# A hybrid attention and mLSTM layer on eight cores: finished mLSTM rows transposed by DMA, from four row buffers

## The chip, the cores and the metric

The kernel runs on the 8 cores of one Trainium2 chip. Each core works through 3 of the 24 sequences alone; the cores share nothing but the memory outside. The metric is the device time in microseconds of the slowest core. A core has TensorE (PE; its weight loads are PEld), VectorE (DVE), ScalarE (ACT), GpSimd (POOL) and SyncE (SP), which here issues nearly all DMAs. Each engine runs its own instructions in order and waits on semaphores for the others.

## The reference

One layer over x of 2048 tokens by 2048 columns per sequence. Cut to what matters:

```python
h = rmsnorm(x, norm_g); proj = h @ w_in            # 6672 columns
# group A: 8 query heads, 2 kv heads, QK norm, rotary positions, softmax attention, times silu(az)
# group B: 4 mLSTM heads, q/k 128 wide, v 256 wide, chunks of 128 tokens, one scan per direction
h_fwd = mlstm_chunkwise(mq, mk, mv, i_f, log_sigmoid(f_f))
h_bwd = flip(mlstm_chunkwise(flip(mq), flip(mk), flip(mv), flip(i_b), flip(log_sigmoid(f_b))))
hm = sigmoid(mo) * (h_fwd + h_bwd)                 # (B, S, 4 heads, 256)
hm = rmsnorm(hm, mlstm_norm_g)                     # per head, weights of 256 columns per head
mlstm_out = hm * silu(mz)
y = concatenate([attn_out, mlstm_out]) @ w_out     # 2048 x 2048
return x + y
```

## The kernel before

A sequence passes through `first_pass` and `attention` (group A), then for each of the 4 mLSTM heads a state stage (`mlstm_states`) and an output stage (`mlstm_out`), then `out_proj`. The normed input stands transposed in `hT`. `mixT` is [128, 16, 2048]: rows 0 to 7 receive the attention output and rows 8 to 15 the mLSTM output, both transposed (column of the mixer on the partition, token along the row), since `out_proj` uses them as stationary operands. The rest of the work uses `arena`, from which tiles are carved by byte offset, and the rows of `mixT` not yet written.

An output stage (L1018 on) runs over 16 chunks c of 128 tokens. Per chunk TensorE computes `front(c+1)` (the scores, L1024, and the forward state update, L1027), `numer(c)` (four matmuls into two banks, L1058 and L1061) and `fin(c)` (the projection to the output gate and the z gate, 16 matmuls of 512 columns, L1094, into bank 6 or 7 by c % 2). Around them:

- VectorE masks the scores (L1032, twice), updates the state (L1043), takes the denominators (L1072 to L1074) and adds the two directions (L1080), all for the numerator; then for the gates L1110 and L1111 (step f1; L1111 is the last reader of the projection's bank), the norm's mean (L1118) and the product of row, norm factor and gate (L1124, step f4) into the row buffer `ob`.
- ScalarE scales the first numerator (L1077, which waits for L1074 and for which L1080 waits), takes the tanh of the projection (L1107, f0), the sum of squares of the gated row into `ob` (L1114, f2, after L1110) and, after the transpose, copies the two halves to `mixT` with the norm's weights `gmcol` as per-partition scale (L1133, f5).
- GpSimd converts the state (L1045) and takes the root (L1120).

What sets the order: the kernel is written out by a planner, the class `Flow`. It holds a clock, `F.now`, which advances by fixed costs when TensorE's work is written (T512 = 217, T256 = 111, T128 = 64 ns), and a list of steps with due times. `F.chain` puts the steps of `fin` at sums of the given distances from the end of its projection; `F.due()`, called ahead of each group of TensorE's work, writes the steps that are due. The order in which instructions are written is the order on each engine, DMAs on SP included. `Sched` (`S`) derives the waits from the tiles read and written; two readers of one PSUM bank count as dependent.

State stages (L932 on) project q, k, v and build the backward states. In the first two sequences those of heads 0 to 2 also carry the prenorm of the next sequence (`prenorm`): SP loads a block of 128 rows of x to one of two buffers `xf` in rows 12 to 15 of `mixT`, nine us later by the planner L450 on ScalarE squares it, and the normed block is stored to `xnd`. Behind L450 on ScalarE stand L954 and L994, which empty the projections' banks. In the first sequence each weight tile is also saved as bf16 (`w_get`, 4 us after its first use) and the next is loaded 1.5 us after the old one is released (`w_rel`).

`out_proj` loads the rows of x to be added into four tiles `xres`, the first four at its start, and writes y through four tiles `ysb`.

Of the kernel before, what the change touches and what calls it, by code (L numbers as in the profile page):

```python
# [7 lines left out]
F32 = mybir.dt.float32  # L8
BF16 = mybir.dt.bfloat16
ALU = mybir.AluOpType  # L10
AF = mybir.ActivationFunctionType
# [202 lines left out]
NT = SEQ // 128  # L214
# [30 lines left out]
T512, T256, T128 = 217.0, 111.0, 64.0  # L245
# [41 lines left out]
def build_program(nseq=SEQ_PER_CORE):  # L287
# [21 lines left out]
    with ExitStack() as es:  # L309
        S = Sched(nc, es)  # L310
        F = Flow()
# [3 lines left out]
        mixT = S.sb("mixT", [128, KC, SEQ], BF16)  # L315
# [27 lines left out]
        def bankb(i):  # L343
            return PP[i // 2].bitcast(BF16)[:, 1024 * (i % 2):1024 * (i % 2) + 1024]
# [4 lines left out]
        def carve(region, off, shape, dt):  # L349
            n = int(np.prod(shape[1:]))  # L350
            nb = n * (4 if dt == F32 else 2)
            base, size = (arflat, ARENA) if region == 'ar' else (mixflat, 65536)
            assert off % 4 == 0 and off + nb <= size, (region, off, nb)
            v = base[:, off // 2:(off + nb) // 2]
            if dt == F32:
                v = v.bitcast(F32)
            if len(shape) == 3:
                v = v.rearrange("p (a b) -> p a b", a=shape[1])
            elif len(shape) == 4:
                v = v.rearrange("p (a b c) -> p a b c", a=shape[1], b=shape[2])  # L360
            return Tile(v, region, off, nb)
# [4 lines left out]
        def mk(r, t0, t1):  # L366
            return ['mx.%d' % (16 * r + t) for t in range(t0, t1)]
# [549 lines left out]
        kxb = [carve('ar', 19968 + 256 * i, [128, 128], BF16) for i in range(4)]  # L917
        Pm = [[carve('ar', 20992 + 512 * i + 256 * d, [128, 128], BF16) for d in range(2)] for i in range(2)]
        Csf = [carve('ar', 22016 + 768 * i, [128, 257], BF16) for i in range(2)]
        ob = [carve('ar', 23552 + 512 * i, [128, 256], BF16) for i in range(2)]  # L920
        soz = [carve('ar', 24576 + 2048 * i, [128, 512], F32) for i in range(2)]
        hA = [carve('ar', 28672 + 1024 * i, [128, 256], F32) for i in range(2)]
        Uf = carve('ar', 39936, [128, 257], F32)
# [2 lines left out]
        def csl(c):  # L926
            return slice(c * 128, (c + 1) * 128)
# [90 lines left out]
        def mlstm_out(s_, h):  # L1018
# [65 lines left out]
            def fin(c):  # L1084
# [26 lines left out]
                    S.op('dve', lambda: V.scalar_tensor_tensor(zo, zo, 1.0, bank(b)[:, 256:512], ALU.add, ALU.mult), reads=[kz, bn], writes=[kz])  # L1111

                def f2():
                    S.op('act', lambda: A.activation(ob[i].ap, oo, AF.Square, accum_out=st[:, 64 + i:65 + i]), reads=[ko],  # L1114
                         writes=[ob[i], 'ssm%d' % i])

                def f3():
                    S.op('dve', lambda: V.tensor_scalar(st[:, 66 + i:67 + i], st[:, 64 + i:65 + i], 1.0 / 64, 16.0 * EPS, ALU.mult, ALU.add),  # L1118
# [2 lines left out]
                         reads=['rlm%d' % i, 'const'], writes=['rsm%d' % i])  # L1121

                def f4():
                    S.op('dve', lambda: V.scalar_tensor_tensor(ob[i].ap, oo, st[:, 68 + i:69 + i], zo, ALU.mult, ALU.mult),  # L1124
                         reads=[ko, kz, 'rsm%d' % i], writes=[ob[i]])

                def f5():
                    tp = bankb(5)
                    S.group('pe', [(lambda k=k: P.transpose(tp[:, 128 * k:128 * k + 128], ob[i].ap[:, 128 * k:128 * k + 128], identb))
                                   for k in range(2)], reads=[ob[i], 'const'], writes=['B5'])  # L1130
                    F.now += 2 * T128
                    for k in range(2):
                        S.op('act', lambda k=k: A.activation(mixT[:, 8 + 2 * h + k, csl(c)], tp[:, 128 * k:128 * k + 128], AF.Copy,  # L1133
                                                             scale=gmcol[:, 2 * h + k:2 * h + k + 1]),
                             reads=['B5', 'constg'], writes=mk(8 + 2 * h + k, c, c + 1))
                F.chain((100, f0), (700 if c > 0 else 1700, f1), (600, f2), (800, f3), (2000, f4), (3600, f5))

            for c in range(NT):
                F.due()
# [5 lines left out]
            w_rel(('OZ%d' % h, s_))  # L1145


        xres = [carve('ar', 30720 + 2048 * i, [128, 512], F32) for i in range(4)]
        ysb = [carve('ar', 2048 * i, [128, 512], F32) for i in range(4)]

        def out_proj(s_):
# [148 lines left out]
```

How the kernel before makes its waits and increments, by code:

```python
    def _wait(self, eng, need):  # L93
        kn = self.known[eng]
        changed = False
        for s, v in need.items():
            if kn.get(s, 0) >= v:
                continue
            if eng == 'pe' and s.startswith('pe_e'):
                continue
            self.E[eng].wait_ge(self.sems[s], v)
            if not changed:
                kn = dict(kn)
                changed = True
            kn[s] = v
            sn = self.snap.get((s, v))
            if sn is not None:
                for s2, v2 in sn.items():
                    if kn.get(s2, 0) < v2:
                        kn[s2] = v2
        if changed:
            self.known[eng] = kn
# [16 lines left out]
    def group(self, eng, fns, reads=(), writes=()):  # L129
        reads, writes = self._bankify(reads, writes)
        self._wait(eng, self._deps(reads, writes))
        sname = "%s_e%d" % (eng, self.epoch[eng])
        sem = self.sem(sname)
        ins = None
        for fn in fns:
            ins = fn()
        ins.then_inc(sem, 1)
        self.cnt[sname] += 1
        ticket = (sname, self.cnt[sname])
        self.snap[ticket] = self.known[eng]
        if self.cnt[sname] >= self.EPOCH:
            self.epoch[eng] += 1
        self._commit(ticket, reads, writes)
        return ticket
# [4 lines left out]
    def dmas(self, eng, pairs, reads=(), writes=(), sem='dma', **kw):  # L149
# [2 lines left out]
        s = self.sem(sem)  # L152
        for (o, i) in pairs:
            self.E[eng].dma_start(out=o, in_=i, **kw).then_inc(s, 16)
            self.cnt[sem] += 16
```

## Time and profile before

| | before |
|---|---|
| median of 3 runs | 4069.55 us (4062.42 to 4496.65) |
| the profiled execution, its own time | 4081.78 us |
| its span on the slowest core (6) | 4080.4 us |
| spans of the 8 cores | 4044.2 to 4080.4 us |
| mean granted TensorE clock of the cores | 0.991 to 0.995 |
| busy: TensorE, VectorE, ScalarE, GpSimd | 96%, 47%, 40%, 23% |
| DMA queue of SP, share of 16 engines | 26.9% |
| L1129, transposes on TensorE | 384, 52.8 us busy |
| L1133, scaled copies on ScalarE | 384, 140.1 us busy |

The profile is of one execution on the slowest core. A line number such as L1094 is the line of the kernel before. Busy time of an engine is the union of its recorded intervals; consecutive instructions overlap, so the distance of two starts says what one costs its engine, and the recorded duration how long it lasts by itself. A wait behind an instruction names who ended the idle time ahead of it.

### The profile page before, as it was taken

Reading aid. Unit: us, or ns where it says so; the run is one execution under the profiler, and the core shown is the slowest. Engines: PE = TensorE matmul, PEld = TensorE weight load, DVE = VectorE, ACT = ScalarE, POOL = GpSimd, SP = SyncE. Lnnn points to the kernel's source line nnn. Section 1 sums busy time; section 2 is a strip of 40 time slices with the busy share of each in tenths; the row PEclk is TensorE's granted clock in tenths of the full one; section 3 lists DMA queues with packets and bytes.
Section 4 is the critical chain, followed back from the end, with each engine's and each line's share of the span. In section 5 each row is a group of like instructions: output and inputs, shape, how many; then the busy total and the mean of one; then the engine's idle time right before and its main releaser. Section 6 shows DMA issues by size and latency. Waiting matters only on the chain.

```text
span 4080.4 us, 72076 instructions; the slowest of 8 cores (4044.2 to 4080.4 us)
## 1 busy us (share of the span) xinstructions
PE 3915.4 (96%) x23590; PEld 2045.7 (50%) x23590; DVE 1928.4 (47%) x4961; ACT 1630.0 (40%) x3479; POOL 947.1 (23%) x1301
## 2 busy tenths in 40 slices
PE   4799899999999999999999999999999999999999
PEld 2444454565554445445456655444544446665544
DVE  3654454455552245445455555224545445555521
ACT  3464456344330026555644433003655563233300
POOL 2443330122210053333021211005333311111100
PEclk8999999999999999999999999999999999999999
DMA  8344410643319931011023211993101100110264
GB/s 220 81 80 67 76 46 20 198 124 110 89 50 219 228 109 30 23 36 36 38 98 120 99 42 47 213 234 92 38 15 35 36 22 22 42 42 22 76 190 149
DMA packets 199342, 358.34 MB, mean 88 GB/s; under 512 B 81088, under 2 KB 130624, under 8 KB 184384
## 3 DMA queue, kind: packets, MB, share of 16 engines
q1 hardware_dynamic: 182768, 318.01, 26.9%
q0 software_dynamic: 16208, 35.72, 6.0%
q8 instruction: 197, 3.23, 0.3%
q14 instruction: 169, 1.38, 0.1%
HBM read 278.25 MB, written 102.76 MB: 93 GB/s over the span
## 4 chain that ended last, share of the span: by engine, by line
PE 83%; DMA 5%; SPq 4%; DVE 3%; issue 3%; ACT 2%; POOL 1%; DVEq 0%; ACTq 0%; POOLq 0%
PE PP L1094 16%; PE PP L1190 12%; PE PP L680 10%; PE PP L762 8%; PE PP L724 8%; PE PP L775 7%; PE PP L947 7%; PE PP L988 6%; SPq L154 4%; PE PP L800 2%; DMA xnd<-arena 1%; DMA arena<-c_rope 1%; PE PP L1058 1%; PE PP L1061 1%; DMA y<-arena 1%
## 5 line engine op out<-in xcount | busy, mean ns | idle before, releaser
L769 ACT ACTIVATE arena<-PP 128x1024 bf16<-128x1024 f32 x768 | 770.4, 1025 | 154.5 <-PE PP L762 153.1
L1094 PE MATMUL PP<-WR,hT 128*128 128x512 bf16 x3072 | 696.2, 379 | 0.2
L1190 PE MATMUL PP<-WR,mixT 128*128 128x512 bf16 x3072 | 669.5, 381 | 9.7 <-DVE arena L1163 9.6
L680 PE MATMUL PP<-WR,hT 128*128 128x512 bf16 (+1 forms) x3072 | 571.5, 328 | 11.1 <-DMA WR<-w_A 9.9
L1190 PEld LDWEIGHTS PP<-WR,mixT 128*128 128x128 bf16 x3072 | 300.8, 98 | 374.8 <-issue 18.7
L762 PE MATMUL PP<-mixT 128*128 128x512 bf16 x1536 | 458.9, 381 | 7.6 <-ACT arena L769 6.4
L775 PE MATMUL PP<-arena,mixT 128*128 128x512 bf16 x1536 | 458.4, 380 | 2.3 <-ACT arena L769 2.3
L1094 PEld LDWEIGHTS PP<-WR,hT 128*128 128x128 bf16 x3072 | 298.7, 98 | 320.5 <-issue 1.0
L724 PE MATMUL PP<-hT,WR 128*128 128x512 bf16 x1536 | 409.8, 382 | 34.7 <-DMA WR<-w_Z 21.9
L680 PEld LDWEIGHTS PP<-WR,hT 128*128 128x128 bf16 x3072 | 298.3, 98 | 244.6 <-issue 15.8
L658 POOL TENSOR_TENSOR mixT<-arena 128x384 f32<-128x384 f32 (+1 forms) x192 | 196.3, 1023 | 907.8 <-DVE arena L639 869.2
L1163 DVE TENSOR_TENSOR arena<-PP,arena 128x512 f32<-128x512 f32 x192 | 132.6, 691 | 517.7 <-PE PP L1190 375.2
L988 PE MATMUL PP<-WR,hT 128*128 128x256 bf16 x3072 | 362.8, 274 | 0.0
L947 PE MATMUL PP<-hT,WR 128*128 128x512 bf16 x1536 | 353.7, 379 | 0.0
L988 PEld LDWEIGHTS PP<-WR,hT 128*128 128x128 bf16 x3072 | 295.4, 98 | 44.2
L649 ACT CAST mixT<-PP 128x128 bf16<-128x128 f32 x96 | 25.6, 266 | 704.5 <-DVE arena L639 677.9
L724 PEld LDWEIGHTS PP<-hT,WR 128*128 128x128 bf16 x1536 | 146.2, 98 | 206.2 <-issue 47.3
L762 PEld LDWEIGHTS PP<-mixT 128*128 128x128 bf16 x1536 | 132.9, 98 | 208.6 <-issue 85.3
L669 POOL TENSOR_TENSOR stats<-stats,ccol 128x3 f32<-128x3 f32 (+1 forms) x192 | 174.4, 909 | 241.8 <-DVE stats L667 239.4
L947 PEld LDWEIGHTS PP<-hT,WR 128*128 128x128 bf16 x1536 | 147.3, 98 | 155.6 <-issue 1.3
L642 ACT ACTIVATE mixT<-PP 128x128 bf16<-128x128 f32 x480 | 134.3, 280 | 203.2 <-DVE arena L639 177.6
L843 POOL TENSOR_TENSOR mixT<-arena 128x512 bf16<-128x512 f32 x90 | 116.8, 1297 | 409.4 <-DVE arena L839 392.4
(156 smaller groups left out, 4438.0 us busy)
## 6 DMA issues: line engine op xcount, KB each, us to landing
arena<-x SPq DMA_DIRECT2D x192, 256.0 KB, 5.0
y<-arena SPq DMA_DIRECT2D x192, 256.0 KB, 5.2
mixT<-x SPq DMA_DIRECT2D x38, 1024.0 KB, 7.0
arena<-c_rope SPq DMA_DIRECT2D x192, 128.0 KB, 2.0
WR<-wd_OUT SPq DMA_DIRECT2D x12, 2048.0 KB, 9.7
xnd<-arena SPq DMA_DIRECT2D x32, 512.0 KB, 2.9
WR<-wd_QKV SPq DMA_DIRECT2D x8, 2048.0 KB, 8.2
WR<-wd_OZ SPq DMA_DIRECT2D x8, 2048.0 KB, 8.1
```

Source lines behind the costliest of these rows:

```text
L154: self.E[eng].dma_start(out=o, in_=i, **kw).then_inc(s, 16)
L658: S.op('pool', lambda: G.tensor_tensor(t23.rearrange("p h (r f e) -> p (h r) f e", r=2, f=2), xrot, tab[r].ap[:, 1:2, :].to_broadcast([128 ...
L669: S.op('pool', lambda: G.tensor_tensor(st[:, c_rs:c_rs + nh], st[:, c_rl:c_rl + nh], nhalf.to_broadcast([128, nh]), ALU.pow), reads=['rlq% ...
L680: S.group('pe', [(lambda kc=kc: P.matmul(pv[:, 0:ncol], hT[:, kc, T * 128:(T + 1) * 128], W[:, kc, c0:c0 + ncol], start=(kc == 0), stop=(k ...
L724: S.group('pe', [(lambda kc=kc: P.matmul(bank(b), W[:, kc, c0:c0 + 128], hT[:, kc, qb * 512:(qb + 1) * 512], start=(kc == 0), stop=(kc == ...
L762: S.group('pe', [(lambda u=u: P.matmul(pr_[:, 512 * u:512 * (u + 1)], kt.ap[:, (2 * j + u) * 128:(2 * j + u + 1) * 128], qt.ap[:, hh, qb * ...
L769: S.op('act', lambda: A.activation(PT[t % NPT].ap, spair[t % 2][:, 0:1024], AF.Exp, scale=128.0 ** -0.5), reads=spn[t % 2], writes=[PT[t % ...
L775: S.group('pe', [(lambda u=u: P.matmul(bank(4), vs.ap[:, 2 * j + u, :], pt.ap[:, 512 * u:512 * (u + 1)], start=(j == 0 and u == 0), stop=( ...
L947: S.group('pe', [(lambda kc=kc: P.matmul(bank(b), W[:, kc, 128 * which:128 * which + 128], hT[:, kc, ts], start=(kc == 0), stop=(kc == KC ...
L988: S.group('pe', [(lambda kc=kc: P.matmul(bank(b)[:, 0:256], hT[:, kc, csl(c)], W[:, kc, 256:512], start=(kc == 0), stop=(kc == KC - 1))) f ...
L1094: S.group('pe', [(lambda kc=kc: P.matmul(bank(b), hT[:, kc, csl(c)], W[:, kc, 0:512], start=(kc == 0), stop=(kc == KC - 1))) for kc in ran ...
L1190: S.group('pe', [(lambda kc=kc: P.matmul(bank(b), mixT[:, kc, csl(T)], W[:, kc, 0:512], start=(kc == 0), stop=(kc == KC - 1))) for kc in r ...
```

## The change

Step f5 no longer transposes on TensorE. It issues two DMA transposes from SP (128x128 each, from the row buffer to the two rows of `mixT`), and no longer multiplies by the norm's weights. A new step f6, once every four chunks, multiplies four chunks of each of the two rows (128x512) in place on ScalarE, 12 us by the planner after the DMAs of the fourth (22 us after those of the last chunk). So that a row can wait for its DMA, the row buffer `ob` has four copies in place of two; the two new ones take bytes 30720 to 31743 of `arena`, and the `xres` tiles of `out_proj` move from 30720 to 8192. f5 is due 0.7 us after f4 (3.6 us before), and the planner's clock no longer advances by 2 x T128 for the transposes.

```diff
-        ob = [carve('ar', 23552 + 512 * i, [128, 256], BF16) for i in range(2)]
+        ob = [carve('ar', o, [128, 256], BF16) for o in (23552, 24064, 30720, 31232)]
...
                 def f2():
-                    S.op('act', lambda: A.activation(ob[i].ap, oo, AF.Square, accum_out=st[:, 64 + i:65 + i]), reads=[ko],
-                         writes=[ob[i], 'ssm%d' % i])
+                    S.op('act', lambda: A.activation(ob[c % 4].ap, oo, AF.Square, accum_out=st[:, 64 + i:65 + i]), reads=[ko],
+                         writes=[ob[c % 4], 'ssm%d' % i])
...
                 def f4():
-                    S.op('dve', lambda: V.scalar_tensor_tensor(ob[i].ap, oo, st[:, 68 + i:69 + i], zo, ALU.mult, ALU.mult),
-                         reads=[ko, kz, 'rsm%d' % i], writes=[ob[i]])
+                    S.op('dve', lambda: V.scalar_tensor_tensor(ob[c % 4].ap, oo, st[:, 68 + i:69 + i], zo, ALU.mult, ALU.mult),
+                         reads=[ko, kz, 'rsm%d' % i], writes=[ob[c % 4]])
 
                 def f5():
-                    tp = bankb(5)
-                    S.group('pe', [(lambda k=k: P.transpose(tp[:, 128 * k:128 * k + 128], ob[i].ap[:, 128 * k:128 * k + 128], identb))
-                                   for k in range(2)], reads=[ob[i], 'const'], writes=['B5'])
-                    F.now += 2 * T128
+                    S.dmas('sp', [(mixT[:, 8 + 2 * h + k, csl(c)], ob[c % 4].ap[:, 128 * k:128 * k + 128]) for k in range(2)],
+                           reads=[ob[c % 4]], writes=mk(8 + 2 * h, c, c + 1) + mk(9 + 2 * h, c, c + 1), sem='ox%d' % (c % 4),
+                           transpose=True)
+
+                def f6():
                     for k in range(2):
-                        S.op('act', lambda k=k: A.activation(mixT[:, 8 + 2 * h + k, csl(c)], tp[:, 128 * k:128 * k + 128], AF.Copy,
-                                                             scale=gmcol[:, 2 * h + k:2 * h + k + 1]),
-                             reads=['B5', 'constg'], writes=mk(8 + 2 * h + k, c, c + 1))
-                F.chain((100, f0), (700 if c > 0 else 1700, f1), (600, f2), (800, f3), (2000, f4), (3600, f5))
+                        row = 8 + 2 * h + k
+                        S.op('act', lambda row=row: A.activation(mixT[:, row, 128 * c - 384:128 * c + 128], mixT[:, row, 128 * c - 384:128 * c + 128],
+                                                                 AF.Copy, scale=gmcol[:, row - 8:row - 7]),
+                             reads=['constg'], writes=mk(row, c - 3, c + 1))
+                F.chain((100, f0), (700 if c > 0 else 1700, f1), (600, f2), (800, f3), (2000, f4), (700, f5), *([(12000 if c < NT - 1 else 22000, f6)] if c % 4 == 3 else []))
...
-        xres = [carve('ar', 30720 + 2048 * i, [128, 512], F32) for i in range(4)]
+        xres = [carve('ar', 8192 + 2048 * i, [128, 512], F32) for i in range(4)]
```

The order on VectorE in the middle of an output stage, before, one chunk (a line number, the operation, output<-input):

```order
L1080 SCALAR_TENSOR_TENSOR arena<-PP,stats,arena 128x256
L1124 SCALAR_TENSOR_TENSOR arena<-arena,stats 128x256
L1032 SCALAR_TENSOR_TENSOR arena<-PP,g_eX,cb 128x128 x2
L1043 SCALAR_TENSOR_TENSOR arena<-arena,g_lam,PP 128x257
L1110 SCALAR_TENSOR_TENSOR arena<-arena 128x256
L1111 SCALAR_TENSOR_TENSOR arena<-arena,PP 128x256
L1072 TENSOR_TENSOR stats<-PP,g_thr 128x2
L1073 SCALAR_TENSOR_TENSOR stats<-PP,stats 128x2
L1074 RECIPROCAL stats<-stats 128x2
L1118 TENSOR_SCALAR stats<-stats 128x1
```

And of the change, at the same place (the lines up to L1129 have the same numbers in both):

```order
L1080 SCALAR_TENSOR_TENSOR arena<-PP,stats,arena 128x256
L1118 TENSOR_SCALAR stats<-stats 128x1
L1032 SCALAR_TENSOR_TENSOR arena<-PP,g_eX,cb 128x128 x2
L1043 SCALAR_TENSOR_TENSOR arena<-arena,g_lam,PP 128x257
L1124 SCALAR_TENSOR_TENSOR arena<-arena,stats 128x256
L1072 TENSOR_TENSOR stats<-PP,g_thr 128x2
L1073 SCALAR_TENSOR_TENSOR stats<-PP,stats 128x2
L1074 RECIPROCAL stats<-stats 128x2
L1110 SCALAR_TENSOR_TENSOR arena<-arena 128x256
L1111 SCALAR_TENSOR_TENSOR arena<-arena,PP 128x256
```

L1124 moved behind the front's three instructions, L1110 and L1111 behind L1072 to L1074, and L1118 behind L1080. The first chunks of a stage have this order in both kernels.

On SP, from the end of head 0's state stage to the first blocks of head 1's in sequence 0, the difference of the two orders (`mixT<-x` is a load of the prenorm, `wd_OZ` and `wd_QKV` are saves of weights):

```order
 L154 DMA xnd<-arena 128x2048 x2
 L154 DMA wd_OZ<-WR 128x8192
+L154 DMA_TRANSPOSE mixT<-arena 128x128 x30
 L154 DMA mixT<-x 128x2048
 L154 DMA wd_QKV<-WR 128x8192
+L154 DMA_TRANSPOSE mixT<-arena 128x128 x2
 L154 DMA mixT<-x 128x2048
 L154 DMA xnd<-arena 128x2048
```

Nothing stood between the save and the two loads of the prenorm before; now the transposes of fifteen chunks stand ahead of the first load and those of the sixteenth ahead of the second.

## Rows read from the trace of the kernel before

**Rows 1.** The page: busy time, share of the span, instructions
```profile
PE 3915.4 (96%) x23590; PEld 2045.7 (50%) x23590; DVE 1928.4 (47%) x4961; ACT 1630.0 (40%) x3479; POOL 947.1 (23%) x1301
```

**Rows 2.** Lines by form: xcount, busy us, mean ns, idle before and releaser
```profile
L1133 ACT ACTIVATE mixT<-PP,gmcol 128x128 bf16<-128x128 bf16 x384 | 140.1, 365 | 65.0 <-PE PP L1129 45.2 <-ACT mixT L1133 0.4
...
L1107 ACT ACTIVATE arena<-PP 128x512 f32<-128x512 f32 x192 | 113.2, 590 | 39.8 <-PE PP L1094 39.7
...
L1114 ACT ACTIVATE arena<-arena 128x256 bf16<-128x256 f32 x192 | 79.9, 416 | 291.2 <-DVE arena L1110 289.4 <-DVE arena L1111 1.8
...
L1129 PE MATMUL PP<-cb,arena 128*128 128x128 bf16 x384 | 52.8, 219 | 0.0
```

**Rows 3.** TensorE in order of time, middle chunk: start, us, instruction
```profile
943.20 0.28 PE L1129 MATMUL PP<-cb,arena 128*128 128x128 bf16 x2
943.31 0.22 PE L1024 MATMUL PP<-arena 128*128 128x128 bf16 x1
...
943.92 3.62 PE L1094 MATMUL PP<-WR,hT 128*128 128x512 bf16 x16
...
948.09 3.62 PE L1094 MATMUL PP<-WR,hT 128*128 128x512 bf16 x16
```

**Rows 4.** VectorE in order of time, middle stretch [idle before <-releaser]
```profile
944.50 0.48 DVE L1080 SCALAR_TENSOR_TENSOR arena<-PP,stats,arena 128x256 f32<-128x256 f32 x1 [0.59 <-ACT arena L1077]
...
948.63 0.49 DVE L1080 SCALAR_TENSOR_TENSOR arena<-PP,stats,arena 128x256 f32<-128x256 f32 x1 [0.59 <-ACT arena L1077]
```

**Rows 5.** VectorE in order of time, early in the same stage
```profile
918.55 0.48 DVE L1080 SCALAR_TENSOR_TENSOR arena<-PP,stats,arena 128x256 f32<-128x256 f32 x1 [0.35 <-ACT arena L1077]
...
920.38 0.48 DVE L1124 SCALAR_TENSOR_TENSOR arena<-arena,stats 128x256 bf16<-128x256 f32 x1
...
921.40 0.42 DVE L1110 SCALAR_TENSOR_TENSOR arena<-arena 128x256 f32<-128x256 f32 x1
921.75 0.41 DVE L1111 SCALAR_TENSOR_TENSOR arena<-arena,PP 128x256 f32<-128x256 f32 x1
922.91 0.48 DVE L1080 SCALAR_TENSOR_TENSOR arena<-PP,stats,arena 128x256 f32<-128x256 f32 x1 [0.74 <-ACT arena L1077]
```

**Rows 6.** ScalarE in order of time, the same early stretch
```profile
921.92 0.42 ACT L1114 ACTIVATE arena<-arena 128x256 bf16<-128x256 f32 x1 [1.98 <-DVE arena L1110]
...
922.34 0.46 ACT L1077 ACTIVATE arena<-PP,stats 128x256 f32<-128x256 f32 x1
```

**Rows 7.** TensorE in order of time, third projection of that stage
```profile
914.69 3.61 PE L1094 MATMUL PP<-WR,hT 128*128 128x512 bf16 x16
```

**Rows 8.** The tensor xnd: ns on SP, min/median/max, and time to landing
```profile
L154 SPq DMA_TRANSPOSE hT<-xnd x32: 2279/5948/12349, 1225.2 to 2713.6; - x32
...
DMA to landing us min/median/max: 2.7/5.4/16.1
```

**Rows 9.** SP in order of time, from 700 us: loads of x rows
```profile
708.72 0.33 SPq L154 DMA_DIRECT2D mixT<-x  x1
...
777.12 0.79 SPq L154 DMA_DIRECT2D mixT<-x  x1
...
801.34 0.43 SPq L154 DMA_DIRECT2D mixT<-x  x1
```

**Rows 10.** DMA issues, 708.7 to 709: KB, us to landing
```profile
mixT<-x SPq DMA_DIRECT2D x1, 1024.0 KB, 26.3
```

**Rows 11.** TensorE in order of time, in head 0's state stage
```profile
741.13 0.26 PE L961 MATMUL PP<-cb,arena 128*128 128x128 bf16 x1 [5.91 <-DVE arena L968]
```

**Rows 12.** State stages: window, length, busy by engine, PEclk, DMA share, GB/s
```profile
709.50:779.20 69.70, 62.25 (x429) 41.30 (x426) 26.65 (x67) 25.79 (x37) 11.53 (x23) 0.95 0.67 199
845.50:906.00 60.50, 59.19 (x423) 39.79 (x421) 24.40 (x66) 26.12 (x44) 10.95 (x22) 1.00 0.59 183
...
2033.60:2098.10 64.50, 59.67 (x429) 39.73 (x426) 26.75 (x68) 25.79 (x37) 11.30 (x22) 1.00 0.43 164
2164.60:2224.60 60.00, 58.98 (x424) 39.98 (x422) 24.19 (x66) 26.13 (x44) 10.44 (x21) 1.00 0.45 167
```

## The prediction

> **What bounds the kernel now.** I read the page first. The reader is to see that TensorE is busy 96% of the span [rows 1]: time goes if TensorE gets less to do, and comes if it is made to wait. Then the grouped lines [rows 2] for the sizes of what is removed, and the engines in order of time in one middle stretch of `mlstm_out`. There TensorE goes from one output projection to the next in 948.09 - 943.92 = 4.17 us without a gap [rows 3]. That is a chunk; there are 16 in a stage, 12 stages (4 heads, 3 sequences), 192 in all. Then VectorE in the same stretch: from one L1080 to the next it takes 948.63 - 944.50 = 4.13 us, and its only idle time is 0.59 us, for ScalarE's L1077 [rows 4]. So VectorE is busy or waiting on a chain of its own all the time, only 0.04 us per chunk ahead of TensorE. That second fact decides the forecast.
>
> **Part 1, the transposes on TensorE go.** Two L1129 start at 943.20 and the next matmul at 943.31 [rows 3]: 0.11 us per chunk, 0.055 each. 384 of them: 384 x 0.055 = 21.1 us of TensorE's time, all on the path. A chunk then needs 4.17 - 0.11 = 4.06 us of TensorE.
>
> The Trainium skill ("TensorE: Matmul & The Clock Gate", Part 4) gives about 275 ns for such a transpose within a kernel, with access latency as most of it; by that the part would be worth 106 us. The trace does not agree: it records 219 ns for one as a duration [rows 2], but the next matmul starts 55 ns later.
>
> **Part 2, ScalarE.** Out go 384 L1133 of 365 ns (140.1 us, [rows 2]); in come 96 scalings of 128x512 from SBUF. Their size isn't in the trace: between 416 ns (L1114, half the elements) and 590 ns (L1107, as many, from PSUM) [rows 2]. I take 590, the nearest in size: 57 us. ScalarE isn't the bound. The two scalings stand behind a tanh (L1107) and ahead of a square (L1114) that waits for VectorE anyway (the 192 L1114 wait 289.4 us for L1110, [rows 2]), so 1.2 us every fourth chunk costs nothing. Without that cover it would be 48 x 1.2 = 57 us of ScalarE, which TensorE sees only past a chunk of lag.
>
> **Part 3, the order on VectorE turns.** The order is made by the planner's clock. With 128 ns less per chunk its chunk is shorter than the 4200 ns to step f4, so L1124 and L1110/L1111 fall behind the next chunk's front (L1032, L1043) and its L1072 to L1074, in every middle chunk. The order rows show it. This order can be priced, because the kernel before runs it once in the first chunks of a stage [rows 5]: L1080, L1118, L1032 twice, L1043, L1124, L1072 to L1074, L1110 (921.40), L1111 (921.75), L1080 (922.91). From L1080 at 918.55 to the next at 922.91 are 4.36 us. Why longer with the same instructions: L1080 waits for ScalarE's L1077, which now stands behind the square L1114, which waits for L1110; so VectorE finishes L1111 and idles 0.74 us where it idled 0.59, and L1118, which used to fill part of the wait before it, comes behind [rows 5, 6]. Nothing in that loop waits for TensorE. So the chain needs 4.36 us per chunk and TensorE 4.06: VectorE falls back 0.30 us per chunk.
>
> What is late next: L1111 frees the PSUM bank that the projection two chunks on writes. In the early stretch it is done at 921.75 + 0.41 = 922.16; without the transposes that projection would start at 914.69 + 2 x 4.06 = 922.81, against 923.03 now [rows 5, 7]. The lead is 0.65 us at the fifth projection, and goes at 0.30 per chunk: it is used up by the seventh. Nine more chunks then run at 4.36: 9 x 0.30 = 2.7 us per stage, 12 x 2.7 = 32 us given back, more than part 1 brought. Bounds: 0, if the records hide slack that I don't see, and 0.30 x 13 = 3.9 per stage (47 us), if no lead is left at chunk 3.
>
> **Part 4, the transposes on the DMA queue.** A DMA transpose from SBUF isn't in the trace; the nearest is `hT<-xnd`, 16 times as large, which holds SP at least 2.28 us [rows 8]. Lower bound for SP: 0.33 us, a plain DMA's issue [rows 9]. If the part above 0.33 goes with size it is 0.33 + 1.95 / 16 = 0.45 us; I take 0.5, so 1 us of SP per chunk of 4.06 to 4.36. For landing I take 3 us, between the bounds 2.7 and 16.1 of `xnd`'s transfers [rows 8] and near the lower, since the queue is nearly empty in an output stage. The row buffer is needed again by L1114 four chunks later. L1114 runs at 921.92 and its L1124 one turn after 920.38, at 924.74 [rows 5, 6], so 4 x 4.36 - 2.8 = 14.6 us remain; the scaling waits for a landing at least 12 us old by the planner. Both are hidden except behind a burst of weights.
>
> The Trainium skill ("VectorE: DVE Perf Modes", The three transpose paths) has 1309 ns for the DMA transpose of 128x128 against 390 ns on TensorE, and its rules say to use TensorE where PSUM will do. By its figure two take 2.6 us of each chunk's 4.06 and the sum stays as it is; no run here shows it yet.
>
> **Part 5, SP is in order.** Before, SP ran ahead: the first two loads of x rows for the next state stage went out at 777.12 and 801.34, tens of us before the stage began at 845.5 [rows 9, 12]. Now each stands behind the transposes of a whole output stage, which wait for L1124; the first goes out just after the state stage begins, the second behind the last chunk's pair, some 5 us in, with the stage's weights (and in sequence 0 the save of weights) ahead of it. The prenorm's L450 on ScalarE waits for them, and behind L450 stand the evictions that TensorE needs. The stage of head 0 shows the price, since there the loads go out that late already: one issued at 708.72 took 26.3 us to land [rows 9, 10], TensorE stood 5.9 us behind it, and the granted clock of the stage was 0.95 in the mean; it took 69.7 us against 60.5 for head 1's [rows 11, 12]. In sequence 1: 64.5 against 60.0 [rows 12]. The change can bring heads 1 and 2 of sequences 0 and 1 to this level: at most 2 x 9.2 + 2 x 4.5 = 27 us, at least 0. I take two thirds of the first and half of the second, because the first load still lands in time: 12 + 4.5 = 16 us. Head 3 and sequence 2 have no such loads.
>
> The move of `xres` makes all four first loads wait for the last numerator matmul; two did so before. They land before the fourth step needs its bank: 0.
>
> **The sum.** -21 + 32 + 16 = +27 us. The profiled execution's own time is 4081.8 (span 4080.4): it would be 4109. The median of the runs shown is 4069.55, 12 us less: forecast 4096 us, 0.6% slower. (2% is 81 us, about what a measurement of this kernel can tell from no change: under 3988 is faster, over 4151 slower.)
>
> **The rivals.**
> - *Only part 3, the x loads stay hidden* (4096 - 16 = 4080). For: the first load has 9 us by the plan. Against: head 0. Chance 0.20.
> - *Neither*: the gain stays, 4069.6 - 21 = 4048. Needs a loop that doesn't reach TensorE; against it is the 4.36 in the trace. Chance 0.14. *Only part 5*: 4064, chance 0.08.
> - *SP becomes the bound*: if a small transpose holds SP as long as the large one's minimum, a chunk needs 2 x 2.28 = 4.56 us of SP; against 4.17 now that is 0.39 x 192 = 75 us, and with part 5 4069.6 + 75 + 16 = 4160, slower by over 2%. It decides from 2.03 us per transpose on (4.06 / 2). Landings over 14.6 us would do the same through L1114. For: each row is a short packet. Against: the large one has 16 times the rows. Chance 0.07.
> - *A transpose is worth its recorded duration*: 384 x 0.219 [rows 2] = 84 us, 3985 us. Against: the 55 ns step. Chance 0.01. The page "TensorE: Matmul & The Clock Gate" of the Trainium skill goes this way, with its 275 ns.
> - The forecast: 0.50, its own range 4072 to 4125.
>
> **How the numbers follow.** Everything but the last two rivals lies within 2%: faster 0.01, same 0.92, slower 0.07. The range goes from the gain kept (4048, and 2 us of scatter) to the forecast with both bounds high (-21 + 47 + 27 = 53: 4123, and 5 us for landings behind the weights): 4046 to 4128. It leaves out the last two rivals, a tail of the forecast and half of *neither*: about 0.17.
>
> **What would show it.** In the profile after: TensorE's chunk 4.06 us at the start of an output stage and about 4.36 at its end, with waits of L1094 or L1058 for L1111 or L1080 of about 0.3 us; VectorE's step from L1080 to L1080 4.36 us with an idle time of 0.74; no wait of L1114 for a DMA in most chunks; SP under 1 us per pair; `mixT<-x` for heads 1 and 2 issued after the stage's start, those stages 63 to 70 us. Wrong would be: chunks of 4.06 us to the end of the stage (part 3 falls), state stages of 60.5 (part 5 falls), or transposes of over 2 us on SP.

## The result, and the profile after

| | before | after |
|---|---|---|
| median of the runs | 4069.55 us | 4144.36 us |
| ratio of the comparable runs, 95% interval | | 1.0162 [1.0129, 1.0194] |
| the profiled execution: span of core 6 | 4080.4 us | 4143.2 us |
| its output stages, 12 together | 796.9 us | 819.9 us |
| its state stages, 12 together | 729.7 us | 768.0 us |
| its attention group, 3 together | 1837.1 us | 1832.0 us |
| its `out_proj`, 3 together | 679.0 us | 685.8 us |

The change made the kernel 1.6% slower, where 0.6% was forecast, and 4144 us lies above the range. Of the three runs after, one (4312.6 us) had a die at a lower clock and is left out of the ratio. A stage is counted from TensorE's first matmul in it to its first in the next, the first attention group from its first projection, the last `out_proj` to TensorE's last matmul.

The table is of the slowest core. From the kernel before to the change, each of the eight cores takes 22.5 to 28.0 us more in its output stages and 25.5 to 38.3 us more in its state stages. In `out_proj` seven cores had 663.9 us before; after, the eight have 663.2 to 694.8.

The page after, busy time of the engines and the chain that ended last, answers [rows 1]:

```profile
PE 3890.5 (94%) x22807; PEld 2018.0 (49%) x23206; DVE 1930.1 (47%) x4961; ACT 1549.4 (37%) x3191; POOL 954.9 (23%) x1301
...
PE 68%; DVE 8%; SPq 7%; issue 7%; DMA 6%; ACT 3%; POOL 1%; DVEq 0%; ACTq 0%; POOLq 0%
```

TensorE has 25 us less to do and stands idle 88 us longer. Three groups of instructions of after, by form (xcount | busy, mean ns | idle before, releaser), answer [rows 2]; the last line is from the same view:

```profile
L1094 PE MATMUL PP<-WR,hT 128*128 128x512 bf16 x2988 | 687.6, 379 | 33.3 <-DVE arena L1111 26.3
...
L1114 ACT ACTIVATE arena<-arena 128x256 bf16<-128x256 f32 x192 | 80.0, 417 | 450.6 <-DVE arena L1110 437.0
...
L1135 ACT ACTIVATE mixT<-mixT,gmcol 128x512 bf16<-128x512 bf16 x96 | 63.7, 714 | 54.5 <-DMA mixT<-arena 54.5
```

The wait of L1094 for L1111 is the forecast one; before, L1094 had 0.2 us of idle time ahead of it in all. TensorE's waits of after (releaser: us, times, longest us) name the second place:

```profile
PE PP L973 <- ACT arena L994: 36.5, 10, 10.3
...
PE PP L1094 <- DVE arena L1111: 26.3, 87, 0.7
```

**Output stage.** TensorE in order of time, head 1 of sequence 0 (start, us; answers [rows 3, 7]):

```profile
933.61 3.62 PE L1094 MATMUL PP<-WR,hT 128*128 128x512 bf16 x15
...
937.67 3.62 PE L1094 MATMUL PP<-WR,hT 128*128 128x512 bf16 x16
...
946.27 3.61 PE L1094 MATMUL PP<-WR,hT 128*128 128x512 bf16 x16 [0.20 <-DVE arena L1111]
...
950.68 3.61 PE L1094 MATMUL PP<-WR,hT 128*128 128x512 bf16 x16 [0.20 <-DVE arena L1111]
```

A chunk takes 937.67 - 933.61 = 4.06 us while TensorE has its lead, and 4.41 once it waits. VectorE over one such chunk (answers [rows 4, 5]) has the forecast order and a slightly larger idle time:

```profile
946.92 0.48 DVE L1080 SCALAR_TENSOR_TENSOR arena<-PP,stats,arena 128x256 f32<-128x256 f32 x1 [0.80 <-ACT arena L1077]
...
949.78 0.42 DVE L1110 SCALAR_TENSOR_TENSOR arena<-arena 128x256 f32<-128x256 f32 x1
950.12 0.41 DVE L1111 SCALAR_TENSOR_TENSOR arena<-arena,PP 128x256 f32<-128x256 f32 x1
951.34 0.48 DVE L1080 SCALAR_TENSOR_TENSOR arena<-PP,stats,arena 128x256 f32<-128x256 f32 x1 [0.80 <-ACT arena L1077]
```

**State stage.** Windows of after: head 1's state stage and output stage in sequence 0, head 1's state stage in sequence 1 (columns as in [rows 12]):

```profile
842.42:917.02 74.60, 60.76 (x414) 40.30 (x417) 24.90 (x68) 27.11 (x45) 11.22 (x22) 0.93 0.67 193
917.02:985.30 68.28, 65.61 (x341) 32.45 (x347) 47.49 (x168) 23.30 (x64) 16.19 (x32) 1.00 0.22 45
2191.68:2260.05 68.37, 61.27 (x414) 40.25 (x418) 24.86 (x68) 27.00 (x45) 10.64 (x21) 0.95 0.44 151
```

They were 60.5, 66.3 and 60.0 us. SP, ScalarE and TensorE around the start of the first of them, in order of time (three answers; SP's rows answer [rows 9]):

```profile
785.83 62.30 SPq L154 DMA_TRANSPOSE mixT<-arena  x30
848.18 0.59 SPq L154 DMA_DIRECT2D mixT<-x  x1
848.88 0.60 SPq L154 DMA_DIRECT2D wd_QKV<-WR  x1
849.57 2.49 SPq L154 DMA_TRANSPOSE mixT<-arena  x2
852.11 1.36 SPq L154 DMA_DIRECT2D mixT<-x  x1
...
865.60 1.91 ACT L450 ACTIVATE arena<-mixT 128x2048 bf16<-128x2048 f32 x1 [12.10 <-DMA mixT<-x]
...
868.00 0.37 PE L973 MATMUL PP<-arena 128*128 128x257 bf16 x1 [10.33 <-ACT arena L994]
```

The first load leaves 5.8 us into the stage and lands some 17 us later; L450 waits for it, L994 stands behind L450, and TensorE behind L994. The save of the QKV weights, at 801 us before, leaves right behind that load.

### The profile page after: what moved, and what is told of

Same layout as the page of the kernel before. It is cut to its first block, busy times and chain, and to the rows that moved or that the text cites. A ratio compares the mean times of both kernels' runs of the same rounds, so it can differ in the third digit from the quotient of the medians.

```text
span 4143.2 us, 70724 instructions; the slowest of 8 cores (4099.1 to 4143.2 us)
## 1 busy us (share of the span) xinstructions
PE 3890.5 (94%) x22807; PEld 2018.0 (49%) x23206; DVE 1930.1 (47%) x4961; ACT 1549.4 (37%) x3191; POOL 954.9 (23%) x1301
## 2 busy tenths in 40 slices
DMA packets 260778, 370.90 MB, mean 90 GB/s; under 512 B 142528, under 2 KB 192064, under 8 KB 245824
## 4 chain that ended last, share of the span: by engine, by line
PE 68%; DVE 8%; SPq 7%; issue 7%; DMA 6%; ACT 3%; POOL 1%; DVEq 0%; ACTq 0%; POOLq 0%
PE PP L680 10%; PE PP L1192 9%; PE PP L1094 9%; PE PP L762 8%; PE PP L724 7%; PE PP L775 7%; SPq L154 7%; PE PP L947 6%; PE PP L988 6%; PE PP L800 2%; DMA mixT<-x 2%; DVE arena L1032 2%; DVE arena L1124 1%; DMA xnd<-arena 1%; DMA arena<-c_rope 1%
## 5 line engine op out<-in xcount | busy, mean ns | idle before, releaser
L1094 PE MATMUL PP<-WR,hT 128*128 128x512 bf16 x2988 | 687.6, 379 | 33.3 <-DVE arena L1111 26.3
L1094 PEld LDWEIGHTS PP<-WR,hT 128*128 128x128 bf16 x3072 | 290.8, 97 | 374.1 <-issue 56.5
L762 PE MATMUL PP<-mixT 128*128 128x512 bf16 x1463 | 441.9, 380 | 15.7 <-ACT arena L769 6.3
L775 PE MATMUL PP<-arena,mixT 128*128 128x512 bf16 x1473 | 444.1, 380 | 5.9 <-ACT arena L769 2.3
L1165 DVE TENSOR_TENSOR arena<-PP,arena 128x512 f32<-128x512 f32 x192 | 132.8, 692 | 523.2 <-DMA y<-arena 262.4
L947 PE MATMUL PP<-hT,WR 128*128 128x512 bf16 x1488 | 353.8, 386 | 2.5
L1114 ACT ACTIVATE arena<-arena 128x256 bf16<-128x256 f32 x192 | 80.0, 417 | 450.6 <-DVE arena L1110 437.0
L947 PEld LDWEIGHTS PP<-hT,WR 128*128 128x128 bf16 x1536 | 150.5, 99 | 166.0 <-issue 11.9
L1120 POOL TENSOR_TENSOR stats<-stats,ccol 128x1 f32<-128x1 f32 x192 | 105.7, 551 | 479.2 <-DVE stats L1118 462.9
```

Of the source, the lines that this page charges most:

```text
L762: S.group('pe', [(lambda u=u: P.matmul(pr_[:, 512 * u:512 * (u + 1)], kt.ap[:, (2 * j + u) * 128:(2 * j + u + 1) * 128], qt.ap[:, hh, qb * ...
L775: S.group('pe', [(lambda u=u: P.matmul(bank(4), vs.ap[:, 2 * j + u, :], pt.ap[:, 512 * u:512 * (u + 1)], start=(j == 0 and u == 0), stop=( ...
L947: S.group('pe', [(lambda kc=kc: P.matmul(bank(b), W[:, kc, 128 * which:128 * which + 128], hT[:, kc, ts], start=(kc == 0), stop=(kc == KC ...
L1094: S.group('pe', [(lambda kc=kc: P.matmul(bank(b), hT[:, kc, csl(c)], W[:, kc, 0:512], start=(kc == 0), stop=(kc == KC - 1))) for kc in ran ...
```

## Experiments

Stage sums below are of core 6 of each profiled execution. The kernel before has 796.9 us in output stages and 729.7 in state stages, of which heads 1 and 2 have 60.5 and 61.1 in sequence 0, 59.9 and 59.7 in sequence 1.

**VectorE's order of before, on the changed kernel.**

```diff
                     transpose=True)
+                    F.now += 2 * T128
...
-                F.chain(... (2000, f4), (700, f5), ... 12000 if c < NT - 1 else 22000, f6
+                F.chain(... (2000, f4), (3600, f5), ... 9100 if c < NT - 1 else 19100, f6
```

> The change with the planner's clock of the kernel before: f5 due 3.6 us after f4 and the clock advanced by 128 ns in f5, f6 2.9 us earlier after f5. VectorE and ScalarE then have exactly the order of before, without L1133. Theory (VectorE's order costs the output stages): each output stage falls from 68.3 us to between 65.5 and 66.2, the 12 together 25 to 33 us, so a ratio to before of about 1.008 in place of 1.016; the state stages of heads 1 and 2 stay long (the loads of x stand behind the transposes still), perhaps a few us better. Rival (the transposes on SP or their transfers cost the output stages by themselves): output stages stay at 68, ratio 1.016.

Ratio 1.0074 [1.0050, 1.0099]. The output stages are 794.3 us together: the whole +23 us of them is gone. The state stages take 747.0, so 17 us of their +38 stay. In sequence 1 they are 61.6 and 59.9, in sequence 0 72.2 and 72.5.

**The order alone, on the kernel before.**

```diff
-                    F.now += 2 * T128
```

> The kernel before, transposes on TensorE, with only the planner's clock not advanced for them: the order on VectorE turns as in the change, SP as before. Theory: VectorE's loop of 4.36 us paces the chunks above TensorE's 4.17, so output stages of 66.3 us grow to 67.5 to 68.8, 12 of them 15 to 30 us, ratio 1.004 to 1.007; state stages unchanged. Rival (the order doesn't matter): ratio 1.000.

Ratio 1.0109 [1.0074, 1.0144]; output stages 818.8 us, 68.2 each, state stages 731.9. The stages are as expected. The ratio is above the expected 1.004 to 1.007: the stages of core 6 add up to 24 us, 0.6%, and the rest lies in the slowest cores of the two longer of its four executions (4116.3 and 4120.0 us; the profiled one took 4091.4). It isn't explained. This kernel issues no DMA transpose in them and its TensorE still does the work of before. VectorE's loop ends as in the change (start, us, idle before):

```profile
949.37 0.48 DVE L1080 SCALAR_TENSOR_TENSOR arena<-PP,stats,arena 128x256 f32<-128x256 f32 x1 [0.75 <-ACT arena L1077]
...
953.74 0.48 DVE L1080 SCALAR_TENSOR_TENSOR arena<-PP,stats,arena 128x256 f32<-128x256 f32 x1 [0.75 <-ACT arena L1077]
```

With the transposes on TensorE and without them the stage takes 68.2 to 68.3 us: once the loop over VectorE and ScalarE sets the chunk, at 4.36 to 4.37 us here, what TensorE is spared doesn't count.

**The planner's clock restored and nothing else.**

```diff
                     transpose=True)
+                    F.now += 2 * T128
```

> The change with one line added: the planner's clock advances by 2 x T128 behind the DMA transposes, as it did behind TensorE's. Nothing else of the work differs. Theory (order on VectorE): the steps fall to other places again, L1124 now directly behind L1118, of which it needs GpSimd's root; each chunk then waits 0.8 us more and takes about 5.2 us, output stages 75 to 79 us, ratio 1.03 to 1.04 above the change, 1.04 to 1.05 above the kernel before. Rival (the DMA transposes or the copies make the output stages long, whatever the order): output stages 68 us as in the change.

The profiled execution took 4253.7 us, 109 more than the change; output stages 78.0 to 78.8 us, 940.2 together. VectorE in order of time there:

```profile
931.45 0.48 DVE L1080 SCALAR_TENSOR_TENSOR arena<-PP,stats,arena 128x256 f32<-128x256 f32 x1 [0.35 <-ACT arena L1077]
931.85 0.14 DVE L1118 TENSOR_SCALAR stats<-stats 128x1 f32<-128x1 f32 x1
932.80 0.48 DVE L1124 SCALAR_TENSOR_TENSOR arena<-arena,stats 128x256 bf16<-128x256 f32 x1 [0.80 <-POOL stats L1120]
...
936.63 0.48 DVE L1080 SCALAR_TENSOR_TENSOR arena<-PP,stats,arena 128x256 f32<-128x256 f32 x1 [0.74 <-ACT arena L1077]
```

L1124 stands behind L1118 and waits 0.80 us for GpSimd's root; the chunk takes 5.18 us. The same instructions in three orders gave output stages of 66, 68 and 78 us. So the order is what sets them.

**The first two loads early**, written 30 us into the output stage ahead (heads 1 and 2, first two sequences).

```diff
...
             W, wk, _ = w_get(('OZ%d' % h, s_))
+            if s_ + 1 < nseq and h < 2:
+                for n in range(2):
+                    F.after(30000 + 100 * n, lambda n=n: xf_load(s_ + 1, n + (6, 11)[h]))
```

> The change, with the first two loads of x for heads 1 and 2 written 30 us into the output stage before (in sequences 0 and 1), so ahead of that stage's last transposes on SP. Theory (late loads cost the state stages): those four state stages fall from 74.6, 73.6, 68.4 and 68.3 us to 60 to 61, together about 43 us, output stages unchanged at 68.3; ratio about 1.006. Rival (the transfers of the transposes slow those stages): they stay at 68 to 75, ratio 1.016.

Ratio 1.0102 [1.0081, 1.0124]; state stages 733.2 us. Sequence 1 is back at 59.9 and 59.5; sequence 0 has 65.9 and 65.2, still 4 to 5 over. So the theory holds in sequence 1 and falls short in sequence 0, and the ratio is above the expected 1.006. Part of that lies in `out_proj`, where the three slowest cores of this run took 669.3 to 674.4 us.

**Both: order of before and early loads.** The two edits above together.

> Both undone: the clock of before and the early loads, transposes still by DMA. Theory: the two repairs add up, -30 and -43 us from the change's +66: ratio 0.997 to 0.999, output stages 65.5 to 66.2, state stages 59 to 61. Rival (something else in the DMA transposes costs 30 us or more): ratio 1.005 or more.

Ratio 1.0070 [1.0048, 1.0092]: not as expected. Output stages 794.2 as they should be, state stages 736.7, since sequence 0 still has 68.3 and 65.3. ScalarE shows a wait there that I had not priced (in this kernel L450 has its old number):

```profile
868.01 1.91 ACT L450 ACTIVATE arena<-mixT 128x2048 bf16<-128x2048 f32 x1 [6.83 <-DMA xnd<-arena]
```

It is the second block's L450, which waits until the first block is stored. That store took 8.8 us to land, 3.9 before. Beside it ran the save of 2 MB, issued 5 us into the stage. The rest of the distance to the kernel before lies in the slowest cores of this run (core 0 has a mean granted clock of 0.984) and isn't explained.

**Loads and save early.** The two edits together, and the save moved as well:

```diff
...
+            if s_ == 0 and nseq > 1 and h < 2:
+                F.after(40000, lambda: w_save(('QKV%d' % (h + 1), 0)))
```

> The change with VectorE's order of before, the first two x loads of heads 1 and 2 written 30 us into the output stage ahead of them, and the save of the QKV weights of heads 1 and 2 written 40 us into it. The run with the loads alone moved kept state stages of 64 to 71 us for heads 1 and 2 of the first sequence, where the kernel before has 60 to 61. Theory: what is left there is the save of 2 MB, which SP issued at 801 us before and issues at 848 us now, beside the load of the next weights and the first stores of the prenorm, so that the second block's L450 waits 7 us for a store. Expected then: state stages of heads 1 and 2 of the first sequence back at 60 to 62 us, the state stages of a core together 724 to 731 us, output stages 65.7 to 66.7 us, ratio to the kernel before 0.997 to 1.001. Rival: the transposes themselves take DMA time from loads and stores; then those two stages stay at 64 to 71 us, the sum at 735 to 745 us, ratio 1.003 to 1.007.

State stages 728.3 us, heads 1 and 2 of sequence 0 at 61.9 and 61.8; output stages 794.0. The 8 cores spanned 4042.6 to 4054.0 us, against 4044.2 to 4080.4 in the profiled execution before. Windows of this run, head 1 of sequence 0, state and output stage:

```profile
833.63:895.56 61.93, 58.83 (x418) 39.73 (x416) 24.33 (x66) 26.68 (x42) 10.97 (x22) 1.00 0.56 165
895.56:961.51 65.95, 65.56 (x350) 32.98 (x349) 47.88 (x168) 24.88 (x66) 15.73 (x32) 1.00 0.40 110
```

The DMA transposes are all still there, so they take no time from loads and stores that TensorE sees. What cost was where they stand in SP's queue. With order, loads and save put right, the change is no slower than the kernel before: its two comparable executions took 4055.1 and 4060.8 us, those of the kernel before beside them 4059.6 to 4088.6. No interval was taken.

**Each DMA transpose twice in head 0's output stages.**

```diff
+                    if h == 0:
+                        S.dmas('sp', [(mixT[:, 10 + k, csl(c)], ob[c % 4].ap[:, 128 * k:128 * k + 128]) for k in range(2)],
+                               ..., sem='oy%d' % (c % 4), transpose=True)
```

> The change, with each DMA transpose of head 0's output stages issued twice (the second pair to rows of mixT that are written later anyhow): four of 1.22 us on SP per chunk, 4.88 us, over the 4.4 us of a chunk. Theory (SP's time per transpose is its own, and SP bounds from 1.1 us per transpose at four, 2.2 us at two): head 0's output stages 76 to 80 us in place of 68.3, the others unchanged, the whole 24 to 36 us longer than the change. Rival (SP's time is a wait for the row and is taken up by the slack of four row buffers): head 0's output stages 68 to 69 us.

Neither. The output stages of head 0 took 71.2, 69.0 and 69.0 us (68.6, 68.6 and 68.3 in the change), the state stages behind them 84.1, 82.0 and 63.5; the whole 4180.6 us in the one execution there is, 36 over the change. SP from 780 to 920 us (ns on SP min/median/max, first and last start):

```profile
L154 SPq DMA_TRANSPOSE mixT<-arena x64: 1180/1233/4211, 787.9 to 877.7; - x64
L154 SPq DMA_DIRECT2D mixT<-x x5: 433/442/735, 871.7 to 903.8; - x5
```

In order of time the sixty transposes ahead of the first load keep SP from 787.9 to 871.7, 83.8 us, where the thirty of the change take 62.3. They start about 1.28 us apart and three of them hold SP for 2.7 to 4.2 us, which makes 5.6 us per chunk of 4.4. SP so ends some 20 us late. The four row buffers take up most of that: the squares L1114 wait for a landing six times, 22.8 us in all, but the stage grows by only 2.5 us. The rest of the debt comes due in the next stage, whose first load leaves at 871.7, 24.9 us after its start and not 5.8. I had priced the rate and forgotten the buffers.

**The norm's weights applied to every chunk by itself.**

```diff
-... mixT[:, row, 128 * c - 384:128 * c + 128] ... if c % 4 == 3
+... mixT[:, row, csl(c)] ... for every c
```

> The change, with the norm's weights applied to every chunk by itself (two copies of 128x128, 12 us behind its DMAs) in place of two of 128x512 every fourth chunk: the same elements, more work on ScalarE (0.82 us per chunk in place of 0.33), which is then idle for some 2.3 us ahead of L1114 in place of 3.1. Theory (L1114 starts 0.58 us behind L1110 after a long idle of ScalarE and 0.52 us after a shorter one, and the loop goes through it): a stalled chunk takes 4.36 us in place of 4.42, output stages 67.5 to 68.1 us in place of 67.9 to 68.6. Rival (more work on ScalarE only lengthens its part of the loop): output stages 68.3 us or more.

The chunk took the expected time, but not for the reason that the theory gives, and the stage did as the rival says. ScalarE in this kernel:

```profile
951.82 0.42 ACT L1114 ACTIVATE arena<-arena 128x256 bf16<-128x256 f32 x1 [2.43 <-DVE arena L1110]
...
956.19 0.42 ACT L1114 ACTIVATE arena<-arena 128x256 bf16<-128x256 f32 x1 [2.43 <-DVE arena L1110]
```

4.37 us from one to the next, where the change takes 4.41 or 4.42 with an idle time of 3.06. The idle time is not what makes the difference. In the change, ScalarE waits for two semaphores ahead of most squares L1114: VectorE's for L1110, and the one that tells that the transposes of four chunks before have left the row buffer. Here a scaling has waited for those transposes already, and in every chunk of this stage but one the square waits for VectorE alone. The last section has the rows. Other chunks took 4.6 to 5.0 us and the output stages 68.2 to 68.8. It gains nothing.

**A better order: the distances 2000, 1600, 800 for f2, f3, f4.**

```diff
-                F.chain(... (600, f2), (800, f3), (2000, f4), (700, f5), ...
+                F.chain(... (2000, f2), (1600, f3), (800, f4), (700, f5), ...
```

Together with the loads and the save moved:

> The change with the two loads and the save moved as in the run beside it, and the distances of the chain 2000, 1600 and 800 for f2, f3 and f4 in place of 600, 800 and 2000, which puts L1118 and L1124 a turn later on VectorE, behind work that does not wait. Theory (the order on VectorE sets the output stage, and TensorE alone bounds a chunk where the order is good, 4.06 us): output stages 64.6 to 65.5 us, state stages as in the run beside it, ratio 0.993 to 0.998. Rival (any order without TensorE's transposes ends at VectorE's and ScalarE's loop): output stages of 66 us and more, ratio 0.999 to 1.003.

> The same kernel as in e6_tuned, timed again. In e6_tuned the undisturbed cores spanned 4022 to 4038 us and those of the kernel before 4040 to 4070 us. Theory: ratio 0.992 to 0.996, output stages 64.6 to 65.0 us. Rival (the gain lies in the noise of the slowest core): interval of the ratio includes 1.

The first timing gave one comparable execution and so no ratio: 4069.3 us, in which six cores took 4022 to 4038 us and two 4063 and 4068 at a granted clock of 0.986 and 0.985. On the second timing the ratio is 0.9944 [0.9918, 0.9969]: this version is faster than both kernels. In the first timing's profile its output stages take 64.6 to 64.9 us (776.6 together). ScalarE in order of time shows why. In this kernel L1094, L1127 and L1131 are what L1077, L1110 and L1114 are in the change:

```profile
936.70 0.47 ACT L1094 ACTIVATE arena<-PP,stats 128x256 f32<-128x256 f32 x1 [1.80 <-DVE stats L1091]
937.40 0.42 ACT L1131 ACTIVATE arena<-arena 128x256 bf16<-128x256 f32 x1 [0.23 <-DVE arena L1128]
```

The scaling of the numerator no longer stands behind the square, so the loop over both engines is cut, and a chunk takes TensorE's own 4.06 us.

The same order on the change without moved loads, and on the kernel before:

> The change with the distances 2000, 1600 and 800 for f2, f3 and f4, no load and no save moved. Theory (order and late loads are two costs that add): output stages 64.6 to 65.0 us, together 777 us per core, state stages as in the change, 750 to 768 us together, so cores of 4055 to 4085 us. Rival (TensorE, faster through the output stages, meets the loads later still): state stages of over 770 us together.

> The kernel before (transposes on TensorE) with the distances 2000, 1600 and 800 for f2, f3 and f4. Theory (the tuned kernel's gain is TensorE's transposes, 2 x 0.055 us in each of 192 chunks): TensorE bounds this one at 4.17 us a chunk as it does the kernel before; output stages 66.0 to 66.8 us, cores of 4040 to 4070 us. Rival (the gain is the order's): output stages of 65.5 us or less.

On the change: output stages 774.0 us, state stages 742.4 (69.6 and 70.2 in sequence 0, 60.3 and 59.7 in sequence 1), cores of 4044.6 to 4074.8. The costs of order and of late loads are two; they don't add quite, for the good order also took most of sequence 1's away (core 3 still has 65.1 and 64.4 there). On the kernel before: output stages of 65.9 to 66.4, cores 4043.1 to 4066.4: no gain to speak of. In the same places it is 66.11 against 64.65 in an output stage and 59.13 against 58.80 in a state stage without loads (core 4 of this run and of the tuned kernel's second profile): 12 x 1.79 = 21 us for the transposes that left TensorE.

## Why the prediction was wrong

On core 6 the output stages (parts 1 and 3) brought +23.0 us where +11 was forecast, the state stages (part 5) +38.3 where 16 was, `out_proj` +6.8 where 0 was, and the attention group -5.1: +63 in place of +27.

- **Part 1** (-21.1 us) holds: 4.06 us a chunk in the profile after, and 21 us between the two kernels in the good order.
- **Part 2** (ScalarE, 0) holds. The scaling of 128x512 took 714 ns, more than the 590 taken, under the same cover.
- **Part 3**: the mechanism and the order are right, and two edits each show it alone. The term was too small: +23.0 net in the output stages where -21 + 32 = +11 was forecast. TensorE's lead ends as forecast, and nine turns of VectorE follow, from L1080 at 942.50 to 982.51. They take 40.0 us, 4.45 each, where I had 4.36. In seven of them the square L1114 starts 0.58 us behind L1110 in place of 0.52, and one has a gap of 0.36 us more between L1032 and L1043. I can't explain that gap, but it isn't the DMA transposes': the order alone on the kernel before has a turn of 4.71 us at the same chunk. I took the loop from [rows 5], where the square waits for VectorE alone. The seven squares wait for a second semaphore, that of the row buffer's transposes, and each such wait makes the loop 0.055 us longer though the transposes landed long before; the two turns without it take 4.36 and 4.37. Nine turns at 4.45 cost 3.5 us per stage, not 2.7, and one more chunk of 4.17 us comes before them.
- **Part 4**: two transposes hold SP for 2.4 us per chunk, not 1; landing takes 2.3 us, not 3. No L1114 stands idle for one, as forecast, and SP isn't the bound of the output stage. What "hidden" left out is the second wait itself, 0.055 us in seven turns of a stage, some 5 us over 12 stages. The scaling stands idle for a landing three times, 54.5 us in all, each in an `out_proj`, where TensorE doesn't wait for it.
- **Part 5** is the step that failed. It forecast 16 us for heads 1 and 2 of sequences 0 and 1 (two thirds of 18.4 and half of 9.0 make 16.8), with 27 as the upper bound. Those four stages took 14.1, 12.5, 8.5 and 8.6 us more, 43.7 together (29.6 on core 0, 28 or more on every core); head 0's stage in sequence 1 took 4.6 us less on core 6, so that the sum of all state stages grew by 38.3 (29.8 on core 0). "The first load still lands in time" is false: it left 5.8 us into the stage and L450 waited 12.1 us for it. Three things were missed. First, the bound. I took head 0's stage as the price of loads that go out "that late already", and they do not: SP issued its first load and its save of weights before the stage began at 709.5, as these rows of before show, and the second load at 708.72 [rows 9]. Nor was head 0's wait the load's alone: it had landed at 735.0, and the L450 at 736.57 was released by the store of the block before it.

```profile
706.31 0.34 SPq L154 DMA_DIRECT2D mixT<-x  x1
706.77 0.36 SPq L154 DMA_DIRECT2D wd_QKV<-WR  x1
```

  In the change the three leave 5.8, 6.5 and 9.7 us after head 1's stage began, some 9 us later within the stage. Second, the save of 2 MB was named and not priced; with order and loads put right it alone held the two stages at 68.3 and 65.3 us, and moving it brought them to 61.9 and 61.8. Third, part 3 feeds part 5: SP waits for the L1124 of chunk 14, which the new order puts a turn later, so the first load leaves at 5.8 us where it leaves at 0.8 with the order of before. In sequence 1 either edit takes the price away: 68.4 and 68.3 us in the change, 61.6 and 59.9 with the order of before, 59.9 and 59.5 with early loads. The tuned order alone does so too (60.3 and 59.7), though its loads leave as late, at 5.0 and 8.8: there the weights leave at 1.9 and 1.5 and the loads land in 7 to 8 us, not 11 to 12, so a late load isn't the cost by itself. In sequence 1 "SP ran ahead" was wrong of the kernel before, too: both loads left 0.5 us and more into the stage, behind its read of weights at 0.1, and that was early enough; the change has them at 5.4 and 9.4, the weights at 4.8.
- `out_proj` was priced at 0, with the move of `xres`. Core 6 has +6.8 us, but it alone was long before (679.0). The other seven had 663.9, and in the change six of the eight have 670.5 to 694.8. On cores 5 to 7 TensorE's waits there are for L1165, and the longest of L1165's for stores of y. The version with loads and save early has 663.2 on every core with the same tiles and transposes, so neither of these costs it by itself; what does stays open.
- The rivals: *SP becomes the bound* is refuted at 1.22 us per transpose, but doubling them shows its true form, a debt that the next stage pays. *Only part 3*, *Neither* and *Only part 5* fall with the output and state stages above.

The Trainium skill ("VectorE: DVE Perf Modes", The three transpose paths) has 1309 ns for the DMA transpose of this size; the runs show 1.22 us on SP and 2.3 to landing. The Trainium skill ("VectorE: DVE Perf Modes", Rules for kernel authors) advises TensorE where PSUM will do; the change as written, 1.6% slower, agrees, and the tuned version, 0.56% faster, does not.

## What to carry to other kernels

When work leaves the engine whose time a planner counts, look first at where every other step lands: here one missing line of the clock cost more than the removed instructions were worth, and another distance turned the loss into a gain. Before putting an instruction that waits for a computation on an in-order DMA queue, list what stood free behind it, loads and saves alike, and issue those first. A queue that falls behind does little harm where the buffers are deep, but much in the next stage that needs a load in time. And count the waits that a moved step adds to a tight loop: here each cost 0.055 us with nothing left to wait for.

## What the runs showed of the hardware

- A DMA transpose of 128x128 bf16 from SBUF to SBUF held SP for 1.09 to 3.85 us, 1.22 in the median, landed 2.3 us after issue in the median and 23 at worst, and made 160 packets (199342 packets on the page before, 260778 after, over 384 transposes).
- A second semaphore wait ahead of an instruction cost ScalarE 0.055 us, though what it waits for was long done. In the change ScalarE waits for VectorE's semaphore alone ahead of the first four squares L1114 of a stage and every fourth after them, and starts 0.52 us behind L1110. Ahead of the others it also waits for the semaphore of the row buffer's transposes, and starts 0.57 to 0.58 us behind it. Three squares of the change, of chunks 3, 6 and 7 (L1110 at 936.58, 949.78 and 954.20; two waits in the middle one alone):

```profile
937.10 0.42 ACT L1114 ACTIVATE arena<-arena 128x256 bf16<-128x256 f32 x1 [3.01 <-DVE arena L1110]
...
950.36 0.42 ACT L1114 ACTIVATE arena<-arena 128x256 bf16<-128x256 f32 x1 [3.06 <-DVE arena L1110]
...
954.72 0.42 ACT L1114 ACTIVATE arena<-arena 128x256 bf16<-128x256 f32 x1 [1.79 <-DVE arena L1110]
```

  It isn't ScalarE's idle time, as I first took it to be. At the same 2.29 us of it, a square with two waits starts 0.57 us behind its L1110 (at 930.00, with the order of before on the change):

```profile
930.57 0.42 ACT L1114 ACTIVATE arena<-arena 128x256 bf16<-128x256 f32 x1 [2.29 <-DVE arena L1110]
```

  One with a single wait starts 0.52 us behind it (at 921.35, the order alone on the kernel before):

```profile
921.87 0.42 ACT L1114 ACTIVATE arena<-arena 128x256 bf16<-128x256 f32 x1 [2.29 <-DVE arena L1110]
```

- A stall costs TensorE more than its length. Windows of after around the 10.3 us wait (columns as in [rows 12]; the granted clock is 0.59, then 0.91):

```profile
860.00:870.30 10.30, 2.29 (x6) 0.90 (x7) 1.82 (x5) 3.79 (x5) 1.33 (x2) 0.59 0.98 310
870.30:880.00 9.70, 9.70 (x61) 6.03 (x60) 2.59 (x7) 2.87 (x4) 1.36 (x3) 0.91 0.82 279
```

  The eight matmuls of L947 behind the wait took 3.62 us, the next eight 2.00: the lower of the two clocks (1.2 GHz) first, then the higher. That is 1.6 us on top of 10.3. What TensorE did before its clock fell was to stand idle, from 857.7 on.
